# A hybrid attention, convolution and expert step: GpSimd multiplies by the final norm's weights, VectorE only scales

## The chip, the cores and the metric

The kernel runs on one core of a Trainium2 chip. The metric is the device time of one execution in microseconds (us). The engines that matter here are TensorE (PE in the profile, with its weight loads as PEld), VectorE (DVE), ScalarE (ACT), GpSimd (POOL) and SyncE (SP). Each runs its own list of instructions in order; they meet only through semaphores.

## The reference

The program is one inference step of a two-layer backbone over 640 tokens (512 latent, 128 context) with 1024 channels. Each layer has attention and a convolution side by side, an output projection, and a grouped mixture of 16 experts. What the change touches is the last line only: a root-mean-square norm of the final tokens, with one weight per channel.

```python
def rmsnorm(x, g):
    xf = x.astype(jnp.float32)
    y = xf * lax.rsqrt(jnp.mean(xf * xf, axis=-1, keepdims=True) + EPS) * g
    return y.astype(x.dtype)

for l in range(DEPTH):
    xs, _, _ = trunk_layer(xs, c, layer(l), router_w, router_b, rope, cache_ckv[:, l], cache_krope[:, l])
y_sample = rmsnorm(xs, final_g)       # and y_prompt = rmsnorm(xp, final_g)
```

## The kernel before, in words

Tokens lie on the 128 partitions. There are five tiles of 128 tokens, each a row block `x[:, t, :]` of 128 x 1024 float32 in SBUF: tiles 0 to 3 are latent, tile 4 is context. Every engine's order is written out by hand, one block of code for each engine; there is no scheduler.

In the expert part of a layer, a loop takes blocks of up to 128 tokens through one expert after another. GpSimd gathers the tokens of a block (L670) and adds the finished block `y_sb` to rows in HBM (L681). The last block of a layer isn't sent through HBM: ScalarE reads the rows back into `x` (L917, one DMA for each tile), TensorE multiplies `y_sb` by a 0/1 matrix so that its rows land at their tokens in PSUM (L1912, "last"), and VectorE adds that to `x`.

After the second layer this end part stands alone, and it is what the change touches. For each tile t in turn:

- VectorE adds two halves of 512 columns (four quarters of 256 for tile 4) from PSUM to `x[:, t, :]`. This is `tt(x..., ALU.add)`, and the profile gives all such helper calls line L935. Each addition frees a PSUM bank and counts up `ring_v.empty`, which the trace shows by the name `dve_bank_empty`.
- ScalarE waits for that count, squares the tile into `junk` with a running sum (L710), takes the root of the mean (L711) and counts up `rms_stat`.
- VectorE, in `normalise(2, t)`, takes the inverse (L1007) and multiplies tile, inverse root and weights in one pass into `xn` (L1012).
- ScalarE waits for `final_ready` and sends the tile out by DMA (L703), one tile's DMA issue standing between the squares of later tiles.

VectorE's written order puts `normalise(2, t - 1)` behind the additions of tile t, so that ScalarE's square of tile t - 1 runs beside the additions of tile t. The weights `final_bc` (the same 1024 values on all partitions) are loaded by ScalarE's queue much earlier. GpSimd has nothing to do in this part: its last instruction is the L681 of its loop's last round. In the profile's names `xn` lies in `region_oq`, `final_bc` and `junk` in `region_bc`, and PSUM is `ps`.

Of the kernel before, what the change touches and what calls it, by code (L numbers as in the profile page):

```python
# [19 lines left out]
ALU = mybir.AluOpType  # L20
# [6 lines left out]
DEPTH = 2  # L27
SEQ, DEC_SEQ, PAST = 128, 512, 128
GRID_W = 64
TILES = (DEC_SEQ + SEQ) // P  # L30
# [132 lines left out]
def hybrid_step_kernel(nc, x_prompt, x_sample, cache_ckv, cache_krope, c, c_ctx, w_ada, b_ada, norm1_g, w_in,  # L163
# [4 lines left out]
    with ctx:  # L168
        def sb(name, cols, dt=FP32, parts=P):
            return ctx.enter_context(nc.sbuf_tensor(name, [parts, cols], dt))  # L170

        def sem(name):
            return ctx.enter_context(nc.semaphore(name))
# [15 lines left out]
        stat = sb("stat", 64)  # L189
# [7 lines left out]
        x = sb("x", TILES * D)[:, :].rearrange("p (t d) -> p t d", t=TILES)  # L197
# [10 lines left out]
        xn = Q[:, :].rearrange("p (t d) -> p t d", t=TILES)  # L208
# [70 lines left out]
        final_bc = bc[:, 1]  # L279
# [17 lines left out]
        ring_v = Ring([ps[:, b] for b in range(4, 8)], sem("dve_bank_full"), sem("dve_bank_empty"))  # L297
# [3 lines left out]
        kvg_loaded, final_loaded = sem("kvg_loaded"), sem("final_loaded")  # L301
# [30 lines left out]
        gu_full, silu_ready, hid_ready = sem("gu_full"), sem("silu_ready"), sem("hid_ready")  # L332
        y_half, y_full, y_taken, y_stored = sem("y_half"), sem("y_full"), sem("y_taken"), sem("y_stored")
        x_stored, x_returned = sem("x_stored"), [sem(f"x_returned{t}") for t in range(TILES)]
        hot_last_ready = sem("hot_last_ready")
        ctx_part_ready, row_gain_ready, blocks_ready = sem("ctx_part_ready"), sem("row_gain_ready"), sem("blocks_ready")

        pool_passed, pe_passed, act_passed = sem("pool_passed"), sem("pe_passed"), sem("act_passed")
        outputs_done, final_ready = sem("outputs_done"), sem("final_ready")
# [3 lines left out]
        def last_parts(t):  # L343
            return 4 if t == LAT else 2
# [204 lines left out]
        def _(pool):  # L549
# [53 lines left out]
            for l in range(DEPTH):  # L603
# [71 lines left out]
                with pool.Fori(0, count - 1) as i:  # L675
# [5 lines left out]
                    pool.indirect_dma_start(x_dram, bass.IndirectOffsetOnAxis(ap=row_out[:, 0:1], axis=0), y_sb, None,  # L681
                                            compute_op=ALU.add).then_inc(y_stored, 16)

# [238 lines left out]
        def _(dve):  # L925
            steps = [0]

            def step(ins):

                steps[0] += 1  # L930
                ins.then_inc(dve_step, 1)
                dve.wait_ge(dve_step, steps[0])
# [71 lines left out]
            def normalise(l, t):  # L1004

                dve.wait_ge(rms_stat, TILES * l + t + 1)
                step(nc.vector.reciprocal(stat[:, 8 + t:9 + t], stat[:, 8 + t:9 + t]))  # L1007
                if l < DEPTH:
                    nc.vector.tensor_scalar(xn[:, t, :], x[:, t, :], stat[:, 8 + t:9 + t], None, ALU.mult).then_inc(xn_ready, 1)
                else:  # L1010
                    dve.wait_ge(final_loaded, 16)
                    nc.vector.scalar_tensor_tensor(xn[:, t, :], x[:, t, :], stat[:, 8 + t:9 + t], final_bc, ALU.mult, ALU.mult).then_inc(final_ready, 1)  # L1012

            for l in range(DEPTH):
                vecs = vec_cols[l]

                if l == 0:
                    for t in range(TILES):
                        normalise(0, t)
                    vector_columns(0)  # L1020
                    ring_v.wait_empty(dve, (0, "vec"))
                    for k in range(DK // 2 + 1, DK, 2):
                        bank = ring_v.take(dve, (l, "xnT", k))
                        nc.vector.tensor_copy(hT[:, k, 0:DEC_SEQ], bank).then_inc(ring_v.empty, 1)
                    bank = ring_v.take(dve, (l, "xpT", 1))
                    nc.vector.tensor_copy(hT[:, 4:8, DEC_SEQ:TOK], bank.rearrange("p (k n) -> p k n", k=4)).then_inc(ring_v.empty, 1)
                    for m in range(1, DEPTH):
                        vector_columns(m)
                        ring_v.wait_empty(dve, (m, "vec"))
                    half_rows(0)  # L1030
                    half_columns(0)
                else:
                    dve.wait_ge(mod_ready, l + 1)
# [402 lines left out]
                for t in range(TILES):  # L1436
                    dve.wait_ge(x_returned[t], 16 * (l + 1))
                    for j in range(last_parts(t)):
                        cols = last_cols(t, j)
                        bank = ring_v.take(dve, (l, "last", t, j))[:, 0:cols.stop - cols.start]  # L1440
                        tt(x[:, t, cols], x[:, t, cols], bank, ALU.add).then_inc(ring_v.empty, 1)
                    if t >= 1:
                        normalise(l + 1, t - 1)
                normalise(l + 1, TILES - 1)


# [494 lines left out]
```

## Time and profile before

| what | value |
|---|---|
| median of 3 runs | 1247.21 us |
| lowest, highest | 1245.6, 1248.94 us |
| profiled execution | 1243.74 us |
| its span, first to last record | 1241.9 us |
| PE, DVE, ACT, POOL busy | 96%, 55%, 33%, 15% of the span |

The span is what the trace covers; the profiled execution's own time is 1.84 us longer, for what lies around it. Times in the rows are from the span's start. A busy share is an average over stages that have different limits, so for the end part one reads the timeline of its last 20 us and not these shares.

### The profile page before, as it was taken

To read this page: it belongs to the slowest core of one execution; us is meant where nothing else is said; L and a number is where in the kernel's file an instruction comes from. 1 tells how busy PE (TensorE), PEld (TensorE's weight loads), DVE (VectorE), ACT (ScalarE), POOL (GpSimd) and SP (SyncE) were. 2 spreads that over 40 slices of the span, in tenths; PEclk is the share of its full clock that TensorE was granted. 3 is DMA by queue.
4 is the path that set the end of the run, shared out by engine and by line. 5 is a ranking of instruction groups with operands and counts; after the bars stand their busy time and mean duration, and the time that the engine had idled before them with its cause. 6 is when DMAs were issued, how large, how long until landed. Compare 5 with 4: busy or idle time off the path is not lost.

```text
span 1241.9 us, 18857 instructions
## 1 busy us (share of the span) xinstructions
PE 1195.2 (96%) x6887; PEld 789.2 (64%) x6888; DVE 688.3 (55%) x1409; ACT 404.4 (33%) x774; POOL 185.5 (15%) x179
## 2 busy tenths in 40 slices
PE   5899999999999999999999999999999999999996
PEld 3444555455544778888876555556664478888884
DVE  3185978565537633333334878786663663333335
ACT  4100213445444222332334003145554321332333
POOL 4000101250300012222210000033110001222220
PEclk9999999999999999999999999999999999999999
DMA  9993430596382749889988000112008165999975
GB/s 326 334 360 138 75 129 1 194 323 237 131 322 85 247 139 352 264 235 339 308 213 231 1 5 1 61 37 99 1 1 295 77 227 160 340 326 330 324 222 187
DMA packets 142075, 238.28 MB, mean 192 GB/s; under 512 B 23266, under 2 KB 106176, under 8 KB 136896
## 3 DMA queue, kind: packets, MB, share of 16 engines
q1 hardware_dynamic: 123936, 186.70, 44.3%
q0 software_dynamic: 11200, 27.69, 9.7%
q10 hardware_dynamic: 6880, 23.09, 4.8%
q8 instruction: 39, 0.64, 0.2%
q14 instruction: 20, 0.16, 0.0%
HBM read 215.06 MB, written 30.77 MB: 198 GB/s over the span
## 4 chain that ended last, share of the span: by engine, by line
PE 87%; DVE 5%; DMA 3%; SPq 2%; issue 2%; ACT 1%; POOLq 0%; ACTq 0%; DVEq 0%
PE ps L1454 52%; PE ps L1717 11%; PE ps L1686 4%; PE ps L1710 3%; PE ps L1480 3%; PE ps L1872 3%; PE ps L1701 2%; DMA region_h<-in_w_ada 1%; PE ps L1912 1%; SPq L471 1%; PE ps L1590 1%; SPq L435 1%; DVE region_h L935 1%; PE ps L1687 1%; DMA region_conv<-h_rows,token_col 1%
## 5 line engine op out<-in xcount | busy, mean ns | idle before, releaser
L1079 DVE SCALAR_TENSOR_TENSOR region_bc<-region_conv,vecs,region_bc 128x655 f32<-128x655 f32 x240 | 202.0, 904 | 0.9
L1454 PEld LDWEIGHTS ps<-region_conv,region_weights 128*128 128x128 f32 x1088 | 124.0, 192 | 9.9 <-issue 7.2
L935 DVE TENSOR_TENSOR region_proj<-ps,region_proj 128x128 f32<-128x128 f32 (+2 forms) x72 | 22.0, 306 | 194.2 <-ACT region_proj L906 165.7
L1454 PEld LDWEIGHTS ps<-region_conv,region_oq 128*128 128x128 f32 x1088 | 124.2, 192 | 8.1 <-issue 8.1
L1454 PE MATMUL ps<-region_conv,region_weights 128*128 128x128 f32 x1088 | 124.4, 275 | 2.3 <-DVE region_conv L1409 2.3
L1454 PE MATMUL ps<-region_conv,region_oq 128*128 128x128 f32 x1088 | 124.2, 275 | 0.0
L1454 PE MATMUL ps<-region_h,region_weights 128*128 128x128 f32 (+1 forms) x432 | 105.5, 405 | 0.0
L906 ACT ACTIVATE region_proj<-ps 128x128 f32<-128x128 f32 x68 | 18.9, 278 | 252.3 <-PE ps L1454 248.2
L1454 PE MATMUL ps<-region_oq 128*128 128x512 f32 (+2 forms) x304 | 94.2, 471 | 2.7 <-issue 2.1
L670 POOL DMA_INDIRECT region_conv<-h_rows,token_col x36 | 38.0, 1056 | 389.4 <-issue 219.5
L1454 PEld LDWEIGHTS ps<-region_h,region_weights 128*128 128x128 f32 x432 | 63.0, 191 | 46.2 <-issue 46.2
L1454 PE MATMUL ps<-region_weights,region_h 128*128 128x512 f32 (+1 forms) x320 | 90.8, 446 | 0.0
L1454 PEld LDWEIGHTS ps<-region_oq 128*128 128x128 f32 x304 | 49.9, 191 | 44.6 <-issue 42.7
L1454 PEld LDWEIGHTS ps<-region_weights,region_h 128*128 128x128 f32 x320 | 52.2, 190 | 39.1 <-issue 39.1
L1686 PE MATMUL ps<-region_weights,region_oq 128*128 128x512 f32 x128 | 71.7, 642 | 4.1 <-ACT region_weights L811 2.5
L1717 PE MATMUL ps<-region_oq,region_proj 128*128 128x512 f32 x160 | 73.1, 600 | 0.0
L1717 PE MATMUL ps<-region_oq,region_h 128*128 128x512 f32 x160 | 71.9, 596 | 0.0
L811 ACT ACTIVATE region_weights<-ps,att_stat 128x640 f32<-128x640 f32 (+1 forms) x80 | 56.4, 708 | 43.0 <-DVE att_stat L1160 42.7
L681 POOL DMA_INDIRECT x_rows<-region_proj,row_out x32 | 50.8, 1588 | 130.7 <-DVE region_proj L1434 130.7
L935 DVE TENSOR_TENSOR region_conv<-ps,region_bc 128x512 f32<-128x512 f32 (+1 forms) x36 | 21.7, 602 | 84.1 <-PE ps L1717 38.0
L1160 DVE TENSOR_REDUCE att_stat<-ps 128x1 f32<-128x640 f32 (+1 forms) x68 | 55.0, 809 | 15.3 <-PE ps L1687 15.3
L1426 DVE SCALAR_TENSOR_TENSOR region_conv<-region_bc,region_proj 128x1024 f32<-128x1024 f32 x34 | 43.7, 1285 | 34.8 <-ACT region_proj L910 34.8
(268 smaller groups left out, 1750.9 us busy)
## 6 DMA issues: line engine op xcount, KB each, us to landing
region_h<-in_w_ada SPq DMA_DIRECT2D x24, 1024.0 KB, 5.0
region_oq<-in_w_ada SPq DMA_DIRECT2D x16, 1024.0 KB, 9.2
region_weights<-in_w_gate SPq DMA_DIRECT2D x16, 1024.0 KB
region_weights<-in_w_up SPq DMA_DIRECT2D x16, 1024.0 KB
region_weights<-in_w_down SPq DMA_DIRECT2D x16, 1024.0 KB
region_oq<-in_w_gate SPq DMA_DIRECT2D x16, 1024.0 KB
region_oq<-in_w_up SPq DMA_DIRECT2D x16, 1024.0 KB
region_oq<-in_w_down SPq DMA_DIRECT2D x16, 1024.0 KB
```

The costliest lines, as they stand in the source:

```text
L670: pool.indirect_dma_start(xg, None, h2_dram, bass.IndirectOffsetOnAxis(ap=token_col[:, 0:1], axis=0), bounds_check=TOK - 1, oob_is_err=Fal ...
L681: pool.indirect_dma_start(x_dram, bass.IndirectOffsetOnAxis(ap=row_out[:, 0:1], axis=0), y_sb, None, compute_op=ALU.add).then_inc(y_stored ...
L811: ins = nc.scalar.activation(prob[:, i % 2, m * P:m * P + n], flat[:, 1024 * (i % 2) + m * P:1024 * (i % 2) + m * P + n], ACT.Exp, bias=s_ ...
L935: return nc.vector.tensor_tensor(out, a, b, op)
L1079: ins = nc.vector.scalar_tensor_tensor(acc[:, ct, :], zpad[:, ct, j:j + CONV_OUT], w, acc[:, ct, :], ALU.mult, ALU.add)
L1160: nc.vector.reduce_max(s_neg[:, cols], src, AXIS_X, negate=True).then_inc(att_max, 1)
L1426: nc.vector.scalar_tensor_tensor(row_gain, g2_bc(0), slot_lat[:, bass.ds(i, 1)], ctx_part, ALU.mult, ALU.add).then_inc(row_gain_ready, 1)
L1454: ins = nc.tensor.matmul(out, lhs(k), rhs(k), start=(k == 0), stop=(k == n - 1))
L1480: ins = nc.tensor.matmul(bank[32 * g:32 * g + 32], cond[:, 32 * k:32 * k + 32], w[:, g * ADA_GROUP:(g + 1) * ADA_GROUP], start=(k == 0), s ...
L1686: nc.tensor.matmul(ps[:, b], q, kT[:, h, 0:512], start=True, stop=True)
L1710: ins = nc.tensor.matmul(ps[hh * VH:(hh + 1) * VH, 6, 0:P], v_sb[:, kt, h * VH:(h + 1) * VH], probT[(2 * g + hh) % 4][:, kt * P:(kt + 1) * ...
L1717: ins = nc.tensor.matmul(bank, (attT if k < 4 else mixT)[:, k, t * P:(t + 1) * P], wout[:, k, j * 512:(j + 1) * 512], start=(k == 0), stop ...
```

## The change

GpSimd gets five multiplications behind its last loop, one for each tile: `xn = x * final_bc`, each after the tile's last addition. A new semaphore `final_gained` counts them. VectorE's last pass becomes a multiplication of `xn`, in place, by the inverse root only; for tile t it waits for `final_gained` to be t + 1. ScalarE's part is as it was.

```diff
@@ gpsimd block, behind the loop of the last layer
+            pool.wait_ge(final_loaded, 16)
+            for t in range(TILES):
+                ring_v.wait_empty(pool, (DEPTH - 1, "last", t, last_parts(t) - 1))
+                nc.gpsimd.tensor_tensor(xn[:, t, :], x[:, t, :], final_bc, ALU.mult).then_inc(final_gained, 1)
@@ vector block, normalise(l, t), the branch for l == DEPTH
-                    dve.wait_ge(final_loaded, 16)
-                    nc.vector.scalar_tensor_tensor(xn[:, t, :], x[:, t, :], stat[:, 8 + t:9 + t], final_bc, ALU.mult, ALU.mult).then_inc(final_ready, 1)
+                    dve.wait_ge(final_gained, t + 1)
+                    nc.vector.tensor_scalar(xn[:, t, :], xn[:, t, :], stat[:, 8 + t:9 + t], None, ALU.mult).then_inc(final_ready, 1)
```

On VectorE, at the start of the end part, the order before is as follows (`x<-x,ps` are the additions; the first row holds those of tiles 0 and 1, and the others go on to tile 1's last pass):

```order
L935 TENSOR_TENSOR x<-x,ps 128x512 x4
L1007 RECIPROCAL stat<-stat 128x1
L1012 SCALAR_TENSOR_TENSOR region_oq<-x,stat,region_bc 128x1024
L935 TENSOR_TENSOR x<-x,ps 128x512 x2
L1007 RECIPROCAL stat<-stat 128x1
L1012 SCALAR_TENSOR_TENSOR region_oq<-x,stat,region_bc 128x1024
```

The same place on VectorE after the change, where line numbers are five higher:

```order
L940 TENSOR_TENSOR x<-x,ps 128x512 x4
L1012 RECIPROCAL stat<-stat 128x1
L1017 TENSOR_SCALAR region_oq<-region_oq,stat 128x1024
L940 TENSOR_TENSOR x<-x,ps 128x512 x2
L1012 RECIPROCAL stat<-stat 128x1
L1017 TENSOR_SCALAR region_oq<-region_oq,stat 128x1024
```

Nothing changes place on VectorE; in each of the five last passes the tensor operand `region_bc` (the weights) is gone, and `x` has become `region_oq` (`xn`).

On GpSimd, the end of the list after the change, with its waits (the first four rows are the loop's last round):

```order
L679 REGISTER_ALU
L681 DMA x_rows<-region_proj,row_out 768x1024 [waits y_taken]
L675 ISA
L675 COMPARE_AND_BRANCH
L687 TENSOR_TENSOR region_oq<-x,region_bc 128x1024 [waits dve_bank_empty,final_loaded]
L687 TENSOR_TENSOR region_oq<-x,region_bc 128x1024 [waits dve_bank_empty] x4
L168 UNCONDITIONAL_BRANCH
```

The two rows of L687 are new: five products stand one behind the other, each with a wait for the additions of its own tile and for nothing else. They do not wait for VectorE's last passes.

## Rows read from the trace of the kernel before

**Rows 1.** The page: busy time by engine, and the chain by engine.
```profile
PE 1195.2 (96%) x6887; PEld 789.2 (64%) x6888; DVE 688.3 (55%) x1409; ACT 404.4 (33%) x774; POOL 185.5 (15%) x179
...
PE 87%; DVE 5%; DMA 3%; SPq 2%; issue 2%; ACT 1%; POOLq 0%; ACTq 0%; DVEq 0%
```

**Rows 2.** Timeline of the end: start, duration (us), engine, line, operation, count, idle before.
```profile
1212.60 1.58 POOL L681 DMA_INDIRECT x_rows<-region_proj,row_out  x1 [2.68 <-DVE region_proj L1434]
...
1224.66 1.48 DVE L935 TENSOR_TENSOR x<-x,ps 128x512 f32<-128x512 f32 x2 [1.35 <-PE ps L1912]
...
1226.38 1.48 DVE L935 TENSOR_TENSOR x<-x,ps 128x512 f32<-128x512 f32 x2 [0.24 <-PE ps L1912]
...
1227.96 1.28 DVE L1012 SCALAR_TENSOR_TENSOR region_oq<-x,stat,region_bc 128x1024 f32<-128x1024 f32 x1
...
1229.17 1.28 DVE L935 TENSOR_TENSOR x<-x,ps 128x512 f32<-128x512 f32 x2
...
1230.55 1.28 DVE L1012 SCALAR_TENSOR_TENSOR region_oq<-x,stat,region_bc 128x1024 f32<-128x1024 f32 x1
...
1233.14 1.28 DVE L1012 SCALAR_TENSOR_TENSOR region_oq<-x,stat,region_bc 128x1024 f32<-128x1024 f32 x1
...
1234.34 1.40 DVE L935 TENSOR_TENSOR x<-x,ps 128x256 f32<-128x256 f32 x4
...
1235.78 1.06 ACT L710 ACTIVATE region_bc<-x 128x1024 f32<-128x1024 f32 x1 [1.24 <-DVE x L935]
1235.85 1.29 DVE L1012 SCALAR_TENSOR_TENSOR region_oq<-x,stat,region_bc 128x1024 f32<-128x1024 f32 x1
...
1236.96 0.29 ACT L711 ACTIVATE stat<-stat,eps_t 128x1 f32<-128x1 f32 x1
...
1237.49 1.29 DVE L1012 SCALAR_TENSOR_TENSOR region_oq<-x,stat,region_bc 128x1024 f32<-128x1024 f32 x1
1238.81 0.34 ACTq L703 DMA_DIRECT2D out_y_prompt<-region_oq  x1
```

**Rows 3.** VectorE's scaling by a column, 128x1024, by its line: min/median/max ns.
```profile
L1009 DVE TENSOR_SCALAR region_oq<-x,stat x10: 753/754/1004, 9.6 to 663.9; 128x1024 f32<-128x1024 f32 x10
```

**Rows 4.** GpSimd's products and sums of 128x655, by line: min/median/max ns.
```profile
L632 POOL TENSOR_TENSOR region_conv<-region_bc x4: 1555/1562/1566, 219.7 to 835.1; 128x655 f32<-128x655 f32 x4
L645 POOL TENSOR_TENSOR region_conv<-region_bc x8: 1278/1344/1416, 257.9 to 870.4; 128x655 f32<-128x655 f32 x8
```

**Rows 5.** Timeline, VectorE's scalings of 128x640 beside GpSimd's products, and one alone.
```profile
256.24 1.59 POOL L644 TENSOR_TENSOR region_bc<-region_bc,region_weights 128x655 f32<-128x655 f32 x1
257.13 1.06 DVE L1168 TENSOR_SCALAR region_weights<-region_weights,att_stat 128x640 f32<-128x640 f32 x1
...
265.54 1.28 POOL L645 TENSOR_TENSOR region_conv<-region_bc 128x655 f32<-128x655 f32 x1
266.15 1.02 DVE L1168 TENSOR_SCALAR region_weights<-region_weights,att_stat 128x640 f32<-128x640 f32 x1
266.90 1.70 POOL L644 TENSOR_TENSOR region_bc<-region_bc,region_weights 128x655 f32<-128x655 f32 x1
...
314.12 6.21 POOL L652 TENSOR_TENSOR region_bc<-region_bc,region_weights 128x655 f32<-128x655 f32 x4 [40.94 <-DVEq L1201]
314.32 1.72 DVE L1168 TENSOR_SCALAR region_weights<-region_weights,att_stat 128x640 f32<-128x640 f32 x1
...
320.77 0.55 DVE L1168 TENSOR_SCALAR region_weights<-region_weights,att_stat 128x640 f32<-128x640 f32 x1
```

**Rows 6.** Timeline, VectorE operations that read PSUM, beside GpSimd's copies and products.
```profile
258.11 0.81 DVE L1160 TENSOR_REDUCE att_stat<-ps 128x1 f32<-128x640 f32 x1
...
809.63 6.08 POOL L627 COPY region_weights<-region_weights 64x768 f32<-64x768 f32 x7 [133.71 <-DVE region_weights L1149]
810.38 0.69 DVE L935 TENSOR_TENSOR region_oq<-ps,con 128x512 f32<-128x512 f32 x1 [0.81 <-PE ps L1454]
```

**Rows 7.** Timeline, a GpSimd operation that waited for VectorE.
```profile
218.65 0.89 DVE L1079 SCALAR_TENSOR_TENSOR region_bc<-region_conv,vecs,region_bc 128x655 f32<-128x655 f32 x1
219.69 3.09 POOL L632 TENSOR_TENSOR region_conv<-region_bc 128x655 f32<-128x655 f32 x2 [17.89 <-DVE region_bc L1079]
```

More of the change, by code:

```diff
@@ L334, in hybrid_step_kernel @@
         x_stored, x_returned = sem("x_stored"), [sem(f"x_returned{t}") for t in range(TILES)]
-        hot_last_ready = sem("hot_last_ready")
+        hot_last_ready, final_gained = sem("hot_last_ready"), sem("final_gained")
         ctx_part_ready, row_gain_ready, blocks_ready = sem("ctx_part_ready"), sem("row_gain_ready"), sem("blocks_ready")
```

## The prediction

> **What bounds the kernel now.** I read the page first. TensorE is busy 96% of the span and carries 87% of the chain that ended last, VectorE 5% of it [rows 1]. That says where the kernel spends its time and nothing about this change, because the change lies wholly behind the last expert product. So the timeline of the last 18 us comes next [rows 2]. There the reader should see VectorE working almost without a pause from 1224.66: additions of a tile (1.28 us from tile 2 on, the wait for TensorE being over), a small inverse, a last pass of 1.28 us, the next tile's additions. A period of a tile is 2.59 us (1227.96 to 1230.55, and 1230.55 to 1233.14). Only the last tile is different: its square can't begin before the additions end (1234.34 + 1.40 = 1235.74), its root ends at 1237.25, its last pass runs from 1237.49 to 1238.78, and the last store is issued at 1238.81. The end of tile 0's additions is at 1224.66 + 1.48 = 1226.14, so the end part takes 1238.78 - 1226.14 = 12.64 us from there. That stretch is what the change can move; the last store and what lies behind it stay as they are. GpSimd ended its last work at 1214.18 and is free.
>
> **What is removed.** Five passes of 1.28 us become scalings by a column. The same operation on the same shape stands in the trace at the first layers' norms: 0.75 us [rows 3]. That is 0.53 us less for each, 2.65 us for all five if nothing else happened. It is the most that the change can give: 0.21% of the time.
>
> **What is added: the products.** GpSimd has no product of 128x1024 in the trace, but many of 128x655. They take 1.28 to 1.57 us where both lines of the group are taken together [rows 4], and I bound by 1.28 below and 1.60 above (1.59 is the longest that stands free of a neighbour's delay, the first of [rows 5]). By 1024/655 this is d = 2.00 to 2.50 us. Four in a row took 6.21 us [rows 5], 1.55 each, and two of those four gave way to VectorE for 0.34 us (below), so 1.38 each without that, or 2.16. I take d = 2.25, the middle. It is near the old period of 2.59 us: GpSimd can just keep up, if it is left alone. How soon a product begins behind an addition: GpSimd's L632 began 0.15 us after VectorE's end (219.54 to 219.69) [rows 7]. VectorE's own last pass begins 0.10 us after its additions end (1230.45 to 1230.55) [rows 2]. For the way back, from a product's end to the scaling, no row shows a wait of VectorE for GpSimd; I take 0.15, as on the way there, with 0.05 and 0.3 as bounds, which matters for one or two tiles only.
>
> The Trainium skill (GPSIMD Engine Reference, section on performance versus the Vector engine) measures a two-input addition of 2048 float32 at 4497 ns, which by half would be an estimate of 2.25 us here. No run here shows a product of that size; by that figure the sum would come out as below.
>
> **What is added: the two engines get in each other's way.** This decides the case. VectorE's scaling of 128x640 takes 0.55 us alone. Beside a GpSimd product it takes 1.06, 1.02, 1.72 us [rows 5], and the ends tell why. The first product ends at 256.24 + 1.59 = 257.83, the scaling at 258.19; the second at 266.82 and 267.17; so each scaling ends 0.35 us after the product, however long before it had begun. The 1.72 us one began 0.2 us into a product and stood through the whole of it. A scaling does not run slower beside a product, it stands still until the product ends, and then does the part of its work in which it streams (640 columns in about 0.35 of its 0.55 us). If a scaling stands waiting when a product ends, it goes first, and the product behind it pays: L644 at 266.90 took 1.70 us. For 1024 columns the free scaling is 0.75 us, and a blocked one ends 0.75 - 0.20 = 0.55 us after the product.
>
> Do the additions stand still too? They read PSUM and one SBUF tensor. An addition of that form took 0.69 us in the midst of GpSimd's seven copies, and a reduction from PSUM 0.81 us beside a product [rows 6]; each is the usual duration of its line. So the additions run freely, and only the last passes are blocked.
>
> **The sum.** Now the order matters. Product 0 begins 0.15 us after tile 0's additions and ends at 0.15 + d, counted from 1226.14. Tile 1's additions have long ended by then (1226.38 + 1.48 = 1227.86), so product 1 follows at once, while scaling 0 only now learns that product 0 is ready. It comes 0.15 us late and stands still through product 1. Behind it on VectorE wait the additions of tile 2, and behind them product 2 and TensorE's last tile. Scaling 0 ends at 0.15 + 2d + 0.55. Additions of tile 2: + 1.21 (they overlap the pass before by 0.07, 1229.17 against 1229.24). Now scaling 1 (its product long ready) comes at + 0.10 and product 2 at + 0.15: nearly a tie. I let the scaling win: + 0.85; then product 2: + d. Tile 3's additions run beside it, so product 3 follows at once and scaling 2 is late again: + d + 0.55. Tile 4's additions: + 1.32 (1234.42 to 1235.74). Scaling 3: + 0.85; product 4: + d; scaling 4: + 0.15 + 0.75. Together 5d + 6.38 us. With d = 2.25 that is 17.63 us against 12.64: 5.0 us slower; with d = 2.0, 3.7 us; with d = 2.5, 6.2 us. ScalarE's root of the last tile (1.51 us behind the additions, 1235.74 to 1237.25) is hidden by product 4, and the stores by the products. If GpSimd wins the ties instead, scaling 1 and 3 stand still too and the chain is 5d + 7.39: 6.0 us slower at d = 2.25, and 4.7 to 7.2 at the bounds. I stay with the first.
>
> On who wins a tie the Trainium skill (SBUF — State Buffer, section on the two separate sides) says that whichever of the two starts first keeps the shared pair of ports for its whole instruction. The rows agree on the standing still; no run here shows a tie, and by that rule the scaling's 0.05 us of lead would give the 5.0.
>
> The sum is made within the profiled execution, 1243.74 us, which would become 1248.7. That execution is 3.5 us below the median of the runs, and a difference carries over: 1247.2 + 5.0 = 1252.2 us.
>
> **Rivals.** (1) The scaling wins at the back-to-back products as well, because the next product is slow to take hold: then products and scalings simply alternate, 0.15 + 5(d + 0.90) = 5d + 4.65 us, 3.3 us slower at 2.25 (2.0 to 4.5). For it: a product can follow another with a gap (the first one ends at 257.83, and its neighbour's scaling, late by then, still went in front of what came next) [rows 5]. Against it: with no one waiting, the way back to VectorE should be longer than that. (2) The other side, not slower: nothing stands still, because what blocks in [rows 5] belongs to those tensors or that form only. Then GpSimd is the bound: five products one behind another, 0.15 + 5d + 0.90 = 12.3 us, where VectorE's new period of about 2.1 us fits beneath it; 0.3 us faster at 2.25, 1.0 faster at d = 2.0 (tile 4's additions then set the start of product 4), 0.9 slower at 2.5. It decides below d = 2.3 us. Every scaling of [rows 5] that met a product speaks against it. (3) The scaling isn't the fast form in place, and takes 1.28 us; it would then probably not be blocked in this way, but it waits for the same products: 0.15 + 5d + 0.15 + 1.28 = 12.8 us or more, from 0 to 2 us slower.
>
> **Chances.** The forecast with its two ways of a tie 0.68, rival (1) 0.16, rival (2) 0.12, rival (3) and anything else 0.04. What can be told from no change is 0.3%, 3.7 us. The forecast passes it except near d = 2.0, some 0.57 of its 0.68, and rival (1) only with a long product, 0.05: slower 0.62. Faster by 3.7 us is excluded by the 2.65 us of the first step, apart from chance between runs: 0.03. The rest, 0.35, is the same. The range: the tie lost with d = 2.5 gives + 7.2, or 1254.4, and runs differ by 1 us or so, hence 1255.2; below, it takes in rival (1) whole and half of rival (2): 1246.9.
>
> **What would show it.** In the profile after, GpSimd has five products of 2.0 to 2.5 us, the first 0.15 us behind tile 0's additions, the second at once behind it. Scaling 0 has a duration of over 2 us and ends about 0.55 us after product 1. At least two of the five scalings are that long and at least one is near 0.75. The additions stay at 0.64 us each. The last store is issued some 17.7 us after tile 0's additions, at the same 0.03 us behind the last scaling. I am wrong if the scalings beside a product take 0.75 us, if the additions grow, or if scaling 0 runs in front of product 1; and the size is wrong if d falls outside its bounds. Nothing ahead of 1223 us should move.

## The result, and the profile after

| what | before | after |
|---|---|---|
| median | 1247.21 us | 1256.6 us |
| profiled execution | 1243.74 us | 1255.81 us |
| its span | 1241.9 us | 1254.0 us |

The ratio is 1.0089 (11.1 us) with a 95% interval of 1.0071 to 1.0107: the changed kernel is slower by 9 to 13 us. The forecast was 5.0 us slower, and its range ended at 1255.2 us.

The timeline of the end, to be laid beside [rows 2] (start, duration, engine, line, operation, count, idle before):

```profile
1225.97 1.48 DVE L940 TENSOR_TENSOR x<-x,ps 128x512 f32<-128x512 f32 x2 [1.35 <-PE ps L1917]
...
1227.60 4.66 POOL L687 TENSOR_TENSOR region_oq<-x,region_bc 128x1024 f32<-128x1024 f32 x2 [11.07 <-DVE x L940]
...
1230.06 2.75 DVE L1017 TENSOR_SCALAR region_oq<-region_oq,stat 128x1024 f32<-128x1024 f32 x1 [0.82 <-POOL region_oq L687]
...
1232.73 1.27 DVE L940 TENSOR_TENSOR x<-x,ps 128x512 f32<-128x512 f32 x2
...
1234.09 2.34 POOL L687 TENSOR_TENSOR region_oq<-x,region_bc 128x1024 f32<-128x1024 f32 x1 [1.83 <-DVE x L940]
1234.11 2.87 DVE L1017 TENSOR_SCALAR region_oq<-region_oq,stat 128x1024 f32<-128x1024 f32 x1
...
1238.26 2.35 POOL L687 TENSOR_TENSOR region_oq<-x,region_bc 128x1024 f32<-128x1024 f32 x1 [1.83 <-DVE x L940]
1238.28 2.87 DVE L1017 TENSOR_SCALAR region_oq<-region_oq,stat 128x1024 f32<-128x1024 f32 x1
...
1242.56 2.35 POOL L687 TENSOR_TENSOR region_oq<-x,region_bc 128x1024 f32<-128x1024 f32 x1 [1.95 <-DVE x L940]
1242.59 2.87 DVE L1017 TENSOR_SCALAR region_oq<-region_oq,stat 128x1024 f32<-128x1024 f32 x1
...
1245.56 0.75 DVE L1017 TENSOR_SCALAR region_oq<-region_oq,stat 128x1024 f32<-128x1024 f32 x1
1246.34 0.34 ACTq L708 DMA_DIRECT2D out_y_prompt<-region_oq  x1
```

The first two additions are tile 0's, and 1227.45 is where they end. Four of five scalings take 2.75 to 2.87 us and only the last, which meets no product, takes 0.75. Each long one ends 0.54 to 0.55 us after a product's end (1236.98 against 1236.43, for one). The additions keep their length (1.27 us for two, 1.28 before). The stretch from the end of tile 0's additions (1227.45) to the issue of the last store (1246.34) is 18.89 us; before it was 1238.81 - 1226.14 = 12.67. That is 6.2 us.

But the span grew by 12.1. Behind the last store's issue lie 1254.0 - 1246.34 = 7.7 us, against 1241.9 - 1238.81 = 3.1. What stands there is not in the timeline of busy engines, since a drain isn't counted as work. It is in the list of the instructions at the end of the program, which all have line L168 (operation, count, min/median/max ns, first and last start). The kernel before:

```profile
L168 POOLq DRAIN  x1: 11259/11259/11259, 1212.5 to 1212.5; - x1
...
L168 SPq DRAIN  x1: 13/13/13, 1241.7 to 1241.7; - x1
```

The kernel after:

```profile
L168 POOLq DRAIN  x1: 11221/11221/11221, 1242.5 to 1242.5; - x1
...
L168 SPq DRAIN  x1: 13/13/13, 1249.7 to 1249.7; - x1
L168 SPq EVENT_SEMAPHORE  x1: 17/17/17, 1253.9 to 1253.9; - x1
```

GpSimd closes its list with a drain of 11.2 us. Before, it ran from 1212.5 to 1223.8, beneath the last expert's work. After, it starts with the last product, at 1242.5, and ends at 1253.7; SyncE, which has seen the last store land at 1249.7, waits another 4.2 us for the others. SyncE's waits say so. The profile names TensorE as the one waited for, because it comes last in the round of signals, though its work had long been done (engine, line, releaser: us, times, longest). Before:

```profile
SPq L168 <- PEq L168: 0.2, 1, 0.2
```

After:

```profile
SPq L168 <- PEq L168: 4.3, 1, 4.3
```

Not all of the 4.6 us is the drain: SyncE's last wait grew by 4.1, and the other 0.5 is the last store itself, which lands 3.1 us after its issue instead of 2.6. That is so in the three kernels here whose last two stores are issued 0.86 us apart (this one and the two below that change only its drains), and 2.6 us in the ten others, where they are 1.6 us or more apart.

So 12.1 us are 6.2 in the end part, 4.6 behind the last store, and 1.3 ahead of the end part (1227.45 against 1226.14). The last isn't the change's. It comes from one place early in the second layer's expert part, where the same 64 matmuls took 7.38 us in the profile before and 9.61 in the one after. They had begun 0.93 us earlier there and took 2.23 longer, which makes the 1.3. Before:

```profile
1036.22 7.38 PE L1454 MATMUL ps<-region_conv,region_weights 128*128 128x128 f32 x64 [1.09 <-DVE region_conv L1409]
```

After:

```profile
1035.29 9.61 PE L1459 MATMUL ps<-region_conv,region_weights 128*128 128x128 f32 x64 [0.88 <-DVE region_conv L1414]
```

TensorE's granted clock in the profile after is 0.50 from 1034 to 1039 us, the lower of its two levels, and 1.00 before and after that; TensorE had stood still for 1.61 us shortly before, waiting for a gather. In the profile before it had stood still for 1.69 us at the same place, and the clock stayed at 1.00. It goes with the execution and not with the change: the same matmuls took 10.25 us in version (a) below, which is no slower than the kernel before, and 7.38 in the changed kernel without drain. The two parts that are the change's, 6.2 + 4.6 = 10.8 us, agree with the 11.1 of the medians.

### The profile page after: what moved, and what is told of

The parts are those of the page before. It is cut to its first block, busy times and chain, and to the rows that moved or that the text cites. A ratio compares the mean times of both kernels' runs of the same rounds, so it can differ in the third digit from the quotient of the medians.

```text
span 1254.0 us, 18863 instructions
## 1 busy us (share of the span) xinstructions
PE 1199.3 (96%) x6887; PEld 792.1 (63%) x6888; DVE 693.8 (55%) x1409; ACT 404.4 (32%) x774; POOL 197.7 (16%) x184
## 4 chain that ended last, share of the span: by engine, by line
PE 86%; DVE 5%; DMA 2%; SPq 2%; issue 2%; ACT 1%; POOL 1%; POOLq 0%; ACTq 0%; DVEq 0%
PE ps L1459 52%; PE ps L1722 11%; PE ps L1691 4%; PE ps L1715 3%; PE ps L1485 3%; PE ps L1877 3%; PE ps L1706 3%; SPq L471 1%; PE ps L1595 1%; SPq L435 1%; DVE region_h L940 1%; PE ps L1692 1%; PE ps L1917 1%; DMA region_h<-in_w_ada 1%; DMA region_conv<-h_rows,token_col 1%
## 5 line engine op out<-in xcount | busy, mean ns | idle before, releaser
L911 ACT ACTIVATE region_proj<-ps 128x128 f32<-128x128 f32 x68 | 18.9, 278 | 254.3 <-PE ps L1459 250.2
```

## The experiments

Theory 1 has two parts: VectorE's scaling and GpSimd's products stand still for each other, and GpSimd's closing drain, about 9 us behind its last work, has come into the open. Theory 2 is that VectorE waits for products that are slow in themselves, and that what lies behind the last store grew for some other reason.

**Without the closing drain.** A block of the program can be told not to drain GpSimd at its end. The edit, to the changed kernel and also, as a control, to the kernel before:

```diff
-        block = ctx.enter_context(nc.Block())
+        block = ctx.enter_context(nc.Block(no_gpsimd_drain=True))
```

Changed kernel without drain:

> The changed kernel, without the drain of GpSimd that closes the program. Theory 1 (GpSimd's drain takes 11.2 us from its last instruction on, and the change starts it at 1242.5 instead of 1212.5, so that it ends 4.3 us after everything else): the part behind the last store shrinks from 7.7 to about 3.3 us, and the time is 4.3 us below the changed kernel's, some 5 to 6 us above the kernel before. Theory 2 (the part behind the last store grew for another reason, such as a later landing of the stores): no difference, 9 to 11 us above the kernel before.

Kernel before without drain:

> The kernel before, without GpSimd's closing drain. Theory 1: that drain was hidden there (1212.5 to 1223.8, with the last store issued at 1238.8), so no difference, within 1 us. Theory 2 says nothing else. If it is faster by more, the drain costs something beyond its place and the comparison of the changed kernel has to be corrected by that.

Measured: ratio 1.0049 (1.0031 to 1.0067), 6.1 us slower than before, for the changed kernel; 0.9999 (0.9983 to 1.0016) for the kernel before. In the first one's profile the last store is issued at 1247.80 and the span ends at 1251.4, 3.6 us later, and the scalings are as long as in the changed kernel (tile 0's additions to the last store 18.9 us). The drain costs the changed kernel some 4 to 5 us, and the kernel before nothing that the runs can tell. What is left agrees with the 6.2 us of the end part and the 0.5 of the later landing, within its interval (4 to 8 us).

**One idle instruction.** The kernel before, and on GpSimd, behind its last loop (the early one waits for tile 0 instead of `LAT`, which is tile 4):

```diff
+            ring_v.wait_empty(pool, (DEPTH - 1, "last", LAT, last_parts(LAT) - 1))
+            nc.gpsimd.memset(idle_col[:, :], 0.0).then_inc(idle_done, 1)
```

Late:

> The kernel before, and GpSimd clears one column of 128 numbers that nobody uses, after the last tile's additions (about 1235.8). No product, nothing that VectorE waits for. Theory 1: the drain begins at about 1235.8 and ends at 1247.1, against 1241.5 for the rest: 5 us slower. Theory 2, and a variant of theory 1 in which the drain's length comes from the products in front of it: within 1 us of the kernel before.

Early:

> As before, but the one column is cleared after the first tile's additions (about 1226.2). Theory 1: the drain ends at 1237.5, ahead of the last store's issue, so nothing is lost: within 1 us of the kernel before. If the mere presence of an instruction costs something, it is some us slower.

Measured: late 1.0025 (1.0013 to 1.0037), 3.1 us slower; early 0.9993 (0.9979 to 1.0007). The clearing and the drain in the late one's profile:

```profile
1236.40 0.10 POOL L686 MEMSET idle_col<- 128x1 f32 x1 [20.50 <-DVE x L939]
```

```profile
L168 POOLq DRAIN  x1: 8954/8954/8954, 1236.4 to 1236.4; - x1
...
L168 SPq DRAIN  x1: 13/13/13, 1242.3 to 1242.3; - x1
```

An instruction of 0.1 us, for which nobody waits, makes the kernel 3 us slower if it comes late, and costs nothing 10 us earlier. Here I had expected 5 us: I took the whole 11.2 us as the drain's own. Its record begins with the instruction in front of it, so the part of its own is 8.95 - 0.1 = 8.85 us, and 11.22 - 2.35 = 8.87 in the changed kernel. The early one's record is as long (8954 ns), though GpSimd had then been idle for 10.0 us and not for 20.5: the price does not shrink with the time since GpSimd's last DMA instruction.

**An early drain.** The changed kernel with

```diff
+            nc.gpsimd.drain()
             pool.wait_ge(final_loaded, 16)
             for t in range(TILES):
```

> The changed kernel with one more drain of GpSimd, between its last loop and the products, where it has some 11 us of idle time. If the closing drain's 8.9 us are work on what the DMAs that GpSimd issued have left behind, the early one does it and the closing one is short: 4 us below the changed kernel. If the 8.9 us are a fixed price of each drain on GpSimd, the closing one is as long as ever and the time is that of the changed kernel, 9 to 11 us above the kernel before.

Measured: 1.0067 (1.005 to 1.0085), 8.3 us slower than before. The two drains of its profile:

```profile
L168 POOLq DRAIN  x1: 2455/2455/2455, 1240.9 to 1240.9; - x1
```

```profile
L684 POOLq DRAIN  x1: 11055/11055/11055, 1214.5 to 1214.5; - x1
```

The closing drain is 0.1 us longer than the product in front of it: the 8.9 us are paid once, by the first drain after the loop of DMAs, and not by each drain. A drain stands at the program's start too, ahead of GpSimd's DMAs and of nearly all its work. In the profile before it is short:

```profile
L1927 POOLq DRAIN  x1: 187/187/187, 0.3 to 0.3; - x1
```

So something that GpSimd did between the start and the end of its loop makes the next drain long. The DMAs are the nearest candidate, but that is not shown: no run leaves them out, and its other operations may have a part.

In the profile the part behind the last store is 3.5 us again (1244.70 to 1248.2). The median kept more than that: 8.3 us against 6.1 without any drain, and the profiled execution (1250.07 us) is the fastest of the four. The intervals (6 to 11 us, and 4 to 8) overlap, and whether an early drain costs a little of its own isn't settled by this run.

**Products that nobody waits for.** The kernel before, without the drain, with five products on GpSimd into the region of old expert weights; VectorE keeps its pass L1012:

```diff
+            pool.wait_ge(final_loaded, 16)
+            for t in range(TILES):
+                ring_v.wait_empty(pool, (DEPTH - 1, "last", t, last_parts(t) - 1))
+                nc.gpsimd.tensor_tensor(W1[:, t * D:(t + 1) * D], x[:, t, :], final_bc, ALU.mult).then_inc(idle_done, 1)
```

> The kernel before, where GpSimd makes the five products as well but into a place that nobody reads, and without GpSimd's closing drain. VectorE keeps its last pass of 1.28 us and waits for no product. Theory 1 (the two engines stand still for each other, whoever needs what): each last pass, which reads two SBUF tensors, stands until the product in course ends and the next product waits for it in turn; worked through with products of 2.35 us, the stretch from tile 0's additions to the last store becomes 17.1 us instead of 12.64, 4.5 us slower. Theory 2 (what costs is that VectorE waits for slow products): no one waits for a product here, so no difference from the kernel before.

Measured: 1.0047 (1.0031 to 1.0064), 5.9 us slower. From its timeline:

```profile
1229.80 15.54 POOL L687 TENSOR_TENSOR region_weights<-x,region_bc 128x1024 f32<-128x1024 f32 x5 [11.71 <-DVE x L940]
...
1231.47 1.78 DVE L1017 SCALAR_TENSOR_TENSOR region_oq<-x,stat,region_bc 128x1024 f32<-128x1024 f32 x1
...
1234.55 2.00 DVE L1017 SCALAR_TENSOR_TENSOR region_oq<-x,stat,region_bc 128x1024 f32<-128x1024 f32 x1
...
1243.26 3.17 DVE L1017 SCALAR_TENSOR_TENSOR region_oq<-x,stat,region_bc 128x1024 f32<-128x1024 f32 x1
1246.46 0.34 ACTq L708 DMA_DIRECT2D out_y_prompt<-region_oq  x1
```

The products one by one (min/median/max ns):

```profile
L687 POOL TENSOR_TENSOR region_weights<-x,region_bc x5: 2367/3331/3347, 1229.8 to 1242.0; 128x1024 f32<-128x1024 f32 x5
```

No data passes from one engine to the other, and still the pass of 1.28 us takes 1.78 to 3.17. The stretch to the last store is 16.8 us (17.1 expected), 4.1 more than before; the five products take 15.54 us together, where alone they would take 11.7. Both sides pay: most products take 3.33 us instead of 2.35, because a pass that already stands waiting when a product ends goes in front of the next one. The first pass ends at 1233.25, 1.08 us after the first product's end (1229.80 + 2.37), and the second product is the longer by nearly that. Theory 2 has no place for this run.

**ScalarE scales.** The changed kernel without drain; ScalarE makes the scaling, so that VectorE has only additions and the inverse:

```diff
-                        act.wait_ge(final_ready, t - 1)
+                        u = t - 2
+                        act.wait_ge(final_root, u + 1)
+                        act.wait_ge(final_gained, u + 1)
+                        step(nc.scalar.activation(xn[:, u, :], xn[:, u, :], ACT.Copy, scale=stat[:, 8 + u:9 + u]))
```

> The changed kernel without the closing drain of GpSimd, where ScalarE instead of VectorE makes the scaling of xn by the inverse root (1.06 us like its squares); VectorE keeps the additions and the small inverse. Theory 1 (standing still): with no operation of VectorE left that is blocked, the products run back to back, 0.1 + 5 x 2.35 = 11.8 us, and one scaling and its way follow: 13.1 us to the last store against 12.64 before and 18.8 in the changed kernel; 0 to 1 us slower than before. Theory 2 (the products are too slow and the wait for them is the cost): it stays near the changed kernel without drain, 5 to 6 us slower.

Measured: 1.0016 (1.0002 to 1.0029), 2.0 us slower. GpSimd and ScalarE in its timeline:

```profile
1226.66 11.61 POOL L687 TENSOR_TENSOR region_oq<-x,region_bc 128x1024 f32<-128x1024 f32 x5 [11.87 <-DVE x L943]
...
1231.19 1.06 ACT L718 ACTIVATE region_bc<-x 128x1024 f32<-128x1024 f32 x1 [0.42 <-DVE x L943]
...
1232.58 1.13 ACT L710 ACTIVATE region_oq<-region_oq,stat 128x1024 f32<-128x1024 f32 x1
1233.74 0.34 ACTq L711 DMA_DIRECT2D out_y_sample<-region_oq  x1
1234.13 1.06 ACT L718 ACTIVATE region_bc<-x 128x1024 f32<-128x1024 f32 x1 [0.42 <-DVE x L943]
```

The same five products now take 11.61 us in a row, 2.32 each. That products are slow in themselves was never the main cost: this kernel is 2.0 us slower than before, where the changed one without drain is 6.1. I had expected 0 to 1 us: the stretch is 14.7 us and not 13.1, since square, root, scaling and issue of a store give ScalarE a period of 2.94 us (1231.19 to 1234.13), which I hadn't added up.

**Alternation by an added wait.** The changed kernel, drain and all:

```diff
                 ring_v.wait_empty(pool, (DEPTH - 1, "last", t, last_parts(t) - 1))
+                if t >= 1:
+                    pool.wait_ge(final_ready, t)
```

> The changed kernel, drain and all, where product t + 1 also waits for the scaling of tile t. Theory 1 (a scaling that comes 0.13 us late is locked out for a whole next product): strict alternation is quicker than what the changed kernel does by itself, 16.5 us to the last store instead of 18.9, no scaling longer than 0.8 us; since the drain starts with the last product, the end moves by 1.8 us: some 8 us above the kernel before and 2 us below the changed one. Rival: an added wait can only cost, and it is as slow as the changed kernel or slower.

Measured: 1.0065 (1.0043 to 1.0087), 8.1 us slower than before where the changed kernel is 11.1. One round of its timeline:

```profile
1232.37 2.35 POOL L689 TENSOR_TENSOR region_oq<-x,region_bc 128x1024 f32<-128x1024 f32 x1 [1.01 <-DVE region_oq L1019]
...
1234.83 0.75 DVE L1019 TENSOR_SCALAR region_oq<-region_oq,stat 128x1024 f32<-128x1024 f32 x1 [1.34 <-POOL region_oq L689]
```

All five scalings take 0.75 us and the stretch is 16.8 us instead of 18.9 (16.5 expected). A wait more, and the end part is 2 us shorter. That gain is read from the profiles; the whole times (5 to 11 us slower here, 9 to 13 for the changed kernel) overlap.

**Versions that might beat both.** (a) GpSimd makes the products of tiles 0 and 1 only, ScalarE scales these two, and VectorE keeps its old pass for tiles 2 to 4; (b) the same with the early drain. The edit on GpSimd is `for t in range(2)` around the products, and on ScalarE that of the kernel above for `u < 2`. (c) No GpSimd: VectorE multiplies tile 4 by the weights while ScalarE squares it, and then scales it:

```diff
+                if l == DEPTH and t == TILES - 1:
+                    dve.wait_ge(final_loaded, 16)
+                    step(nc.vector.tensor_tensor(xn[:, t, :], x[:, t, :], final_bc, ALU.mult))
                 dve.wait_ge(rms_stat, TILES * l + t + 1)
```

(a):

> A version that follows from the runs so far: GpSimd makes the products of tiles 0 and 1 only, ScalarE scales these two, VectorE keeps its old pass for tiles 2, 3 and 4. Nothing of VectorE but the pass of tile 2 can meet a product, and only its last 0.4 us. With the durations of the changed kernel's trace (products 2.35, additions 1.28, pass 1.28, ScalarE 1.06 to 1.14) the last store is issued 10.6 us after tile 0's additions instead of 12.64. GpSimd's drain ends 2.4 + 2.35 + 8.9 = 13.7 us after them, the last store lands at about 13.3: 1.5 to 2 us faster than before if the theory of standing still and of the drain is right, 0.12 to 0.16%. If a product costs by its mere presence, it is slower.

(b):

> The same with an early drain of GpSimd between its loop and the products, as in the earlier run with an early drain. The closing drain is then under 3 us and hidden by far. If the early drain costs nothing by itself, 2 us faster than before, at most 0.5 us from the version without it; if it delays the last scatter's landing or the reading back of the rows, some of that is lost.

(c):

> The change's own idea on VectorE alone and for tile 4 only: VectorE multiplies the last tile by the weights (1.28 us) while ScalarE squares it (1.51 us to its root), and then scales it in 0.75 us; GpSimd does nothing. The stretch behind tile 4's additions shrinks from 3.04 to 2.5 us: 0.5 us faster than before, 0.04%, below what the runs can tell; the profile must show the scaling at 0.75 us and no idle time of VectorE over 0.2 us ahead of it.

Measured: (a) 0.9999 (0.9987 to 1.0011), (b) 0.9999 (0.9987 to 1.0011), (c) 1.001 (0.9991 to 1.0028). None beats the kernel before. In (a) the stretch is 12.2 us, 0.4 less than before and not 2: the two scalings push ScalarE's squares of tiles 2 and 3 back, as in the kernel where it makes all five. Its GpSimd drain ends at 1241.9 and is covered. In (c) the end of tile 4's additions to the last store's issue became 3.55 us from 3.07:

```profile
1236.16 1.28 DVE L1018 SCALAR_TENSOR_TENSOR region_oq<-x,stat,region_bc 128x1024 f32<-128x1024 f32 x1
...
1237.36 1.22 DVE L1008 TENSOR_TENSOR region_oq<-x,region_bc 128x1024 f32<-128x1024 f32 x1
...
1238.82 0.75 DVE L1015 TENSOR_SCALAR region_oq<-region_oq,stat 128x1024 f32<-128x1024 f32 x1
```

I had forgotten that VectorE still has tile 3's pass to make in that time; the product of tile 4 comes behind it and is late. (b) gives the same time as (a), so that an early drain costs nothing that these runs can tell; its closing drain ends 0.1 us after the last product (1235.2).

## Why the prediction was wrong, point by point

- **Direction.** Right, and for the mechanism given: the scalings stand still beside products and end 0.55 us after them. It accounts for somewhat more than half of the 11.1 us.
- **The step that failed: "the last store and what lies behind it stay as they are".** They grew by 4.6 us, 4.1 of them the wait for GpSimd's closing drain and 0.5 a later landing of the last store. The prediction gave GpSimd's list five products and asked only who waits for them. It did not ask what stands behind them on GpSimd: the row of its branch out of the loop was shown, and behind it comes a drain of 8.9 us beyond the last instruction, which all engines' common end waits for. The run without drain (4 to 5 us less) and the idle instruction (3 us more, with nothing else changed) show this cause by itself. Nothing in the busy times showed it before; the list of the closing instructions did, with its 11259 ns from 1212.5 on.
- **The tie.** "I let the scaling win" was wrong. The product won all three ties, by 0.02 to 0.03 us (1234.09 against 1234.11): it began 0.08 to 0.09 us behind the additions and not the 0.15 that I had from another place [rows 7], and the scaling 0.11 behind them. The other branch, named with 5d + 7.39 us, gives 19.1 us with the measured d; measured are 18.9. It cost 1.0 us of the sum, and makes four long scalings where I expected two.
- **d.** 2.35 us against 2.25, within 2.00 to 2.50. Over five products 0.5 us. The Trainium skill's figure (GPSIMD Engine Reference, performance versus the Vector engine), halved an estimate of 2.25 us, is 4% below it.
- **Steps that held.** Scaling alone 0.75 us; product 1 at once behind product 0, and scaling 0 too late, by 0.13 us (0.15 taken); additions untouched; 0.55 us of a blocked scaling behind the product. Together 5.0 + 0.5 + 1.0 would have been 6.5 us, and the end part did grow by 6.2, or 6.1 by the run without drain.
- **Rival (1)** is what the added wait enforces: 5d + 4.65 is 16.4 us, and 16.8 were measured. **Rival (2)** is refuted by the four long scalings of the changed kernel itself, and by the run in which nobody waits for the products. **Rival (3)** is refuted by the last scaling, in place and 0.75 us long.
- **"Nothing ahead of 1223 us should move"** did not hold: the profile is 1.3 us late there. The cause is the granted clock at 1035 us, not the change.

## What to carry to other kernels

Work given to an idle engine at the end of a program also moves that engine's closing instructions: ask what its list has behind the new work, above all on GpSimd, and read the closing lines of the profile as well as the busy ones. Two engines that block each other whole instruction by whole instruction make a share of work dearer than its length; check first whether the receiving engine's work and the giving engine's remaining work can run at the same time at all. Where one of them runs back to back and the other comes a tenth of a microsecond late, an added wait that forces them to alternate can be a gain (2 us of the end part here, not enough to beat the kernel before).

## What the runs showed of the hardware that I had not expected

- A drain of GpSimd after a loop of gathers and scattered additions takes 8.85 to 8.9 us beyond the instruction in front of it (8.95 us with a clearing of 0.1 us, 11.22 us with a product of 2.35 us in front), and a second one 0.1 us. Directly behind the last scattered addition, as in the kernel before, it is 9.6 us (1214.18 to 1223.8). The drain at the program's start takes 0.19 us.
- VectorE's pass with two SBUF inputs (1.28 us) is blocked as its scaling is: 1.78 to 3.17 us beside products. The Trainium skill (SBUF — State Buffer, the two separate sides) says that a VectorE instruction with two SBUF inputs and a GpSimd one that reads SBUF exclude each other, and that the one which starts later is fully blocked. The runs agree, and add that a VectorE instruction which stands waiting goes in front of the next GpSimd one (five products in 15.54 us with such passes in between, 11.61 without).
